# Low-part subtractions moved in attention and in the second recurrence, and a half square moved from VectorE to ScalarE and Pool

## The chip, the cores and the metric

The kernel runs on one NeuronCore of a Trainium2 chip. The metric is the device time of one execution in microseconds, and lower is better. Engines are named as in the profile: PE is TensorE (PEld its weight loads), DVE is VectorE, ACT is ScalarE, POOL is GpSimd, and SP is the queue that issues the weight loads.

## What is computed

The reference is a decoder trunk for 256 tokens of width 1024, all in float32. It has two layers:

```
x = x + rg_lru_block(rmsnorm(x))        # conv, gates, recurrence, output projection
x = x + swiglu(rmsnorm(x))              # dense, width 2816
k, v, c = shared_kv(rmsnorm(x))         # keys, values, summed log forget gates
x = x + fox_attention(rmsnorm(x), k, v, c)   # 16 heads of 64, causal, sigmoid output gate
x = x + moe(rmsnorm(x))                 # top 2 of 8 experts, width 3584
return rmsnorm(x)
```

The recurrence is h[t] = a[t] h[t-1] + b[t] for each of 1024 channels. rmsnorm divides each token by the root of its mean square plus 1e-6. Attention computes, for each head, softmax(q.k / 8 + c[t] - c[s]) over the past, times v, times the gate.

## The kernel before

**Weights in units.** All weight matrices are read as units of 1 MB (128 partitions x 2048 columns), numbered in the order in which TensorE uses them. SP loads unit u into one of six slots of raw. To keep float32 precision with the fast matmul type, every product is made of three: ScalarE rounds the unit to w_hi (split_hi, L400), VectorE makes w_lo = raw - w_hi (split_lo, L751), and TensorE multiplies low by high, high by low and high by high (mm3, L1284 to L1286). w_hi and w_lo have three slots. Activations are split in the same way (act_hi, act_lo, alt_hi, alt_lo).

**Order.** There is no planner. Each engine has its own instruction list, written out by hand, and works through it in order; semaphores join the lists. split_lo(u) waits until ScalarE's count hi_done has reached u + 1, that is until split_hi(u) is done. SP loads unit u + 6 when split_lo(u) is done (lo_done). TensorE starts a unit when its w_lo is there.

**The recurrent block** (units 0 to 11). VectorE handles the eight chunks of channels in two halves. recurrence(h) makes the input of the scan with two elementwise instructions (L892, L894) and runs four scans (L896). After recurrence(1) VectorE runs split_lo(9), then multiplies the result with the gate (gated, L854), with split_lo(10), the low parts (gated_lo, L859), some small constants, split_lo(11) and split_lo(12). Units 8 to 11 are the output projection; TensorE takes units 8 and 9 whole, and units 10 and 11 in two parts, token block 0 first.

**The norm between stages, n = 1 and n = 2.** The 256 tokens are two blocks of 128. For block 1 VectorE adds the first half of the row (add_half, L806), squares and sums it (block1_first_half), takes low parts of block 0 (block_lo, L773), adds the second half, and squares and sums that on top (block1_second_half, L778). Pool raises the mean square to the power -1/2 (inverse_rms, L334). ScalarE scales the second half row (scale_half, L424) and VectorE the first (block1_scale, L802). TensorE transposes the scaled block (transpose_block, L1374), ScalarE rounds it (block_hi, L419) and VectorE makes its low parts. Stage n = 1 leads into the dense layer, n = 2 into keys and values.

**Attention.** Eight passes i = 0 to 7, two heads each, with this list for each engine:

```
PE:   logits(i), transpose_probs(i-1), gate_half(i), values(i-1)
ACT:  out_gate(i-1), probs_T(i-1), exps(i), heads_hi(i-2), split_hi(U_G+2+i/2) if i is even
DVE:  gated_heads(i-2), maxima(i), norms(i), heads_lo(i-2), split_lo(U_G+2+i/2) if i is even
```

maxima (L1046) adds the mask and takes row maxima, exps (L602) exponentiates and sums, norms (L1053, L1056) divides by the sum, transpose_probs (L1541) turns the probabilities, probs_T (L595) copies them to SBUF, values (L1563) multiplies by v, gated_heads (L1067) applies the gate. norms(i) waits for p_exp of its pass, transpose_probs(i) waits for p_norm, probs_T(i) for pt_done. gate_half is half a unit of the gate projection and fills TensorE meanwhile. The units split in attention are U_G+2 to U_G+5; the last two of these belong to the output projection, U_O and U_O+1.

Of the kernel before, what the change touches and what calls it, by code (L numbers as in the profile page):

```python
# [18 lines left out]
D = 1024  # L19
# [8 lines left out]
EPS = 1e-6  # L28
# [8 lines left out]
HALF = D // 2  # L37
# [32 lines left out]
def yoco_kernel(nc, x_in, norm_g, lru_w_in, lru_conv_w, lru_conv_b, lru_gate_w, lru_gate_b, lru_lambda,  # L70
# [6 lines left out]
    with ctx:  # L77
# [117 lines left out]
        ms_ready, rms_ready, xs_act_ready, w_part, d_part, hT_done = (sem(n) for n in ("ms_ready", "rms_ready", "xs_act_ready", "w_part", "d_part", "hT_done"))  # L195
        norm_T, act_hi_done, act_lo_done = sem("norm_T"), sem("act_hi_done"), sem("act_lo_done")
# [116 lines left out]
        def _(pool):  # L313
# [17 lines left out]
            def inverse_rms(n):  # L331
                for t in range(NT):
                    pool.wait_ge(ms_ready, 2 * (n - 1) + t + 1)
                    g.tensor_tensor(rstd[:, n, t:t + 1], msq[:, n, t:t + 1], neghalf[:, 0:1], ALU.pow).then_inc(rms_ready, 1)  # L334
# [59 lines left out]
        def _(act):  # L394
# [18 lines left out]
            def block_hi(n, t, gain, hi):  # L413

                for c in range(KD):
                    if c % 2 == 0:
                        act.wait_ge(norm_T, 4 + 8 * (n - 1) + 4 * t + c // 2 + 1)
                    lo = (c % 2) * T + t * P
                    a.activation(hi[:, c, t * P:(t + 1) * P], bank[4 + c // 2][:, lo:lo + P], ACT.Copy,  # L419
                                 scale=cols[:, gain + c:gain + c + 1]).then_inc(act_hi_done, 1)  # L420

# [101 lines left out]
            block_hi(1, 0, R_NORM + KD, act_hi)  # L523
            scale_half(1)
# [31 lines left out]
            block_hi(2, 0, R_KVN, alt_hi)  # L556
            split_hi(U_V + 2)
# [181 lines left out]
        def _(dve):  # L739
# [37 lines left out]
            def mean_square(n, t, part, so_far, into, count_sem=None):  # L777
                ins = v.tensor_tensor_reduce(out=xs[:, t, part], in0=x[:, t, part], in1=x[:, t, part], scale=1.0 / D, scalar=so_far,  # L778
                                             op0=ALU.mult, op1=ALU.add, accum_out=into)
                if count_sem is None:  # L780
                    link(ins)
                else:
                    ins.then_inc(count_sem, 1)

            def block0_norm(n):

                dve.wait_ge(x_added, 4 * (n - 1) + 2)
                mean_square(n, 0, slice(0, D), EPS, msq[:, n, 0:1], ms_ready)
                dve.wait_ge(rms_ready, 2 * n - 1)
                v.tensor_scalar(xs[:, 0, :], x[:, 0, :], rstd[:, n, 0:1], None, ALU.mult).then_inc(xs_ready, 1)  # L790

            def block1_first_half(n):
                dve.wait_ge(x_added, 4 * (n - 1) + 3)
                mean_square(n, 1, slice(0, HALF), EPS, ss[:, n, 1:2])

            def block1_second_half(n):
                dve.wait_ge(x_added, 4 * (n - 1) + 4)
                mean_square(n, 1, slice(HALF, D), ss[:, n, 1:2], msq[:, n, 1:2], ms_ready)
# [89 lines left out]
            def recurrence(h):  # L888
# [5 lines left out]
                link(v.tensor_tensor(xc[:, part, :], rc[:, part, :], xc[:, part, :], ALU.mult))  # L894
                for c in range(4 * h, 4 * h + 4):
                    last = v.tensor_tensor_scan(rc[:, c, :], decay[:, c, :], xc[:, c, :], 0.0, ALU.mult, ALU.add)  # L896
# [26 lines left out]
            recurrence(1)  # L923
            split_lo(9)
# [30 lines left out]
            block1_second_half(1)  # L955
# [42 lines left out]
            block1_second_half(2)  # L998
# [76 lines left out]
            for i in range(NPH):  # L1075
                if i >= 2:
                    gated_heads(i - 2)
                maxima(i)
                norms(i)
                if i >= 2:  # L1080
                    heads_lo(i - 2)
                if i % 2 == 0:
                    split_lo(U_G + 2 + i // 2)
# [684 lines left out]
```

## Time and profile before

| | |
|---|---|
| median of 3 runs | 1418.53 us (1417.25 to 1419.8) |
| profiled execution, its own time | 1418.73 us |
| its span | 1417.0 us |
| PE busy | 1389.7 us, 98% |
| DVE busy | 1123.2 us, 79% |
| ACT busy | 937.2 us, 66% |
| POOL busy | 55.5 us, 4% |

The profile is that of one execution. Its span runs from the first to the last instruction, and the execution's own time is 1.73 us longer. A row of a timeline gives start and duration in microseconds, the engine, the line of the kernel, the operation, the tile written and the tiles read, and in brackets the idle time of the engine ahead of it with what ended it. Matmuls are pipelined and their ends are modelled, so a row of PE can be longer than the distance to the next one.

### The profile page before, as it was taken

The numbers are of one execution on the slowest core, as the hardware profiler recorded it, in microseconds if no ns is written. First come the engines' busy times: TensorE is split into PE (matmuls) and PEld (weight loads), VectorE is DVE, ScalarE is ACT, GpSimd is POOL, SyncE is SP. The second block draws the span as 40 slices with busy tenths as digits, with TensorE's granted clock in tenths as the row PEclk, the third lists the DMA queues.
The fourth block names the chain that finished last, engine by engine and source line by source line (L and its number), as shares of the span: only waits on it lengthen the run. The fifth ranks groups of instructions, "written<-read, shape, count | busy, mean of one in ns | idle before, by whom it ended". The sixth has DMA issues, their size and how long they took to land.

```text
span 1417.0 us, 19751 instructions
## 1 busy us (share of the span) xinstructions
PE 1389.7 (98%) x7327; PEld 1190.2 (84%) x7327; DVE 1123.2 (79%) x878; ACT 937.2 (66%) x738; POOL 55.5 (4%) x77
## 2 busy tenths in 40 slices
PE   8989999999999999999999999999999999999997
PEld 7979999979878888888788888888888888888885
DVE  7885445576657988888898888888889888888995
ACT  5853343354656777777777777777777777777773
POOL 2002000002003000000000000000000000003000
PEclk9999999999998999999999999999999999999999
DMA  9547955659343999999999999999999999999991
GB/s 311 198 147 270 354 181 192 190 164 384 136 147 113 409 408 393 381 397 365 350 402 367 357 412 376 366 371 406 375 358 402 379 354 407 381 378 369 413 394 64
DMA packets 147772, 454.26 MB, mean 321 GB/s; under 512 B 7528, under 2 KB 50640, under 8 KB 133360
## 3 DMA queue, kind: packets, MB, share of 16 engines
q1 hardware_dynamic: 139360, 423.65, 80.0%
q0 software_dynamic: 6144, 22.12, 4.1%
q10 hardware_dynamic: 2192, 7.39, 1.3%
q8 instruction: 58, 0.95, 0.3%
q14 instruction: 18, 0.15, 0.0%
HBM read 429.54 MB, written 23.59 MB: 320 GB/s over the span
## 4 chain that ended last, share of the span: by engine, by line
PE 92%; DVE 3%; ACT 3%; issue 1%; DMA 0%; ACTq 0%; DVEq 0%; POOLq 0%; POOL 0%
PE bank L1284 29%; PE bank L1285 29%; PE bank L1286 29%; PE bank L1681 2%; DVE w_lo L751 1%; ACT prob L602 1%; ACT w_hi L400 1%; PE bank L1355 0%; PE bank L1689 0%; DMA rows<-in_lru_lambda 0%; DVE rc L896 0%; PE bank L1541 0%; DVE act_lo L773 0%; PE bank L1633 0%; PE bank L1397 0%
## 5 line engine op out<-in xcount | busy, mean ns | idle before, releaser
L1183 DVE TENSOR_TENSOR w_lo<-raw,w_hi 128x2048 fp32r<-128x2048 f32 x249 | 566.3, 2290 | 73.8 <-ACT w_hi L676 72.4
L676 ACT ACTIVATE w_hi<-raw 128x2048 fp32r<-128x2048 f32 x249 | 475.0, 1917 | 142.2 <-PE bank L1286 132.1
L1284 PE MATMUL bank<-w_hi,act_lo 128*128 128x512 f32 (+1 forms) x752 | 291.6, 388 | 3.4 <-issue 1.4
L1286 PE MATMUL bank<-w_hi,act_hi 128*128 128x512 f32 (+1 forms) x752 | 290.0, 386 | 0.0
L1285 PE MATMUL bank<-w_lo,act_hi 128*128 128x512 f32 (+1 forms) x752 | 289.6, 385 | 0.0
L751 DVE TENSOR_TENSOR w_lo<-raw,w_hi 128x2048 fp32r<-128x2048 f32 x67 | 153.2, 2290 | 96.4 <-ACT w_hi L400 96.3
L1183 DVE TENSOR_TENSOR alt_lo<-raw,alt_hi 128x2048 fp32r<-128x2048 f32 x84 | 192.4, 2290 | 37.4 <-ACT alt_hi L676 36.6
L676 ACT ACTIVATE alt_hi<-raw 128x2048 fp32r<-128x2048 f32 x84 | 161.0, 1917 | 43.4 <-PE bank L1286 38.8
L1284 PEld LDWEIGHTS bank<-w_hi,act_lo 128*128 128x128 f32 x752 | 141.9, 189 | 32.9 <-issue 3.3
L1284 PE MATMUL bank<-act_hi,w_lo 128*128 128x256 f32 x576 | 164.8, 286 | 1.9 <-DVE act_lo L763 1.9
L1286 PEld LDWEIGHTS bank<-w_hi,act_hi 128*128 128x128 f32 x752 | 141.5, 188 | 28.4
L1285 PEld LDWEIGHTS bank<-w_lo,act_hi 128*128 128x128 f32 x752 | 141.7, 188 | 27.7
L1285 PE MATMUL bank<-act_lo,w_hi 128*128 128x256 f32 x576 | 162.9, 283 | 0.0
L1286 PE MATMUL bank<-act_hi,w_hi 128*128 128x256 f32 x576 | 162.9, 283 | 0.0
L400 ACT ACTIVATE w_hi<-raw 128x2048 fp32r<-128x2048 f32 x67 | 128.0, 1912 | 38.4 <-PE bank L1286 38.4
L1284 PE MATMUL bank<-w_hi,hid_lo 128*128 128x512 f32 x376 | 148.5, 395 | 0.0
L1285 PE MATMUL bank<-w_lo,hid_hi 128*128 128x512 f32 x376 | 147.8, 393 | 0.0
L1286 PE MATMUL bank<-w_hi,hid_hi 128*128 128x512 f32 x376 | 146.7, 390 | 0.0
L1284 PEld LDWEIGHTS bank<-act_hi,w_lo 128*128 128x128 f32 x576 | 109.9, 191 | 3.1 <-issue 1.5
L1285 PEld LDWEIGHTS bank<-act_lo,w_hi 128*128 128x128 f32 x576 | 109.9, 191 | 0.5
L1286 PEld LDWEIGHTS bank<-act_hi,w_hi 128*128 128x128 f32 x576 | 109.9, 191 | 0.0
L1284 PE MATMUL bank<-alt_hi,act_lo 128*128 128x512 f32 x240 | 94.5, 394 | 0.0
(283 smaller groups left out, 1675.9 us busy)
## 6 DMA issues: line engine op xcount, KB each, us to landing
raw<-in_moe_w_gu SPq DMA_DIRECT2D x224, 1024.0 KB, 7.6
raw<-in_moe_w_down SPq DMA_DIRECT2D x112, 1024.0 KB, 7.8
raw<-in_mlp_w_gu SPq DMA_DIRECT2D x22, 1024.0 KB, 5.2
raw<-in_mlp_w_down SPq DMA_DIRECT2D x11, 1024.0 KB, 5.0
raw<-in_lru_w_in SPq DMA_DIRECT2D x8, 1024.0 KB, 12.7
tok_rows<-zeros POOLq DMA_DIRECT2D x16, 512.0 KB, 17.2
raw<-in_w_kvf SPq DMA_DIRECT2D x8, 1024.0 KB, 5.4
raw<-in_fox_w_qg SPq DMA_DIRECT2D x8, 1024.0 KB, 5.5
```

What stands on the lines that cost most here:

```text
L400: a.activation(w_hi[:, u % SPL, :], raw[:, u % RAW, :], ACT.Copy).then_inc(hi_done, 1)
L602: a.activation(prob[:, b, cut], prob[:, b, cut], ACT.Exp, scale=-1.0, bias=negmax[:, b, t:t + 1], accum_out=psums[:, b, t:t + 1]).then_inc ...
L676: a.activation(moe_slot(g)[0], raw[:, u % RAW, :], ACT.Copy).then_inc(hi_done, 1)
L751: v.tensor_tensor(w_lo[:, u % SPL, :], raw[:, u % RAW, :], w_hi[:, u % SPL, :].bitcast(f32), ALU.subtract).then_inc(lo_done, 1)
L1183: v.tensor_tensor(lo, raw[:, u % RAW, :], hi.bitcast(f32), ALU.subtract).then_inc(lo_done, 1)
L1284: t_.matmul(dst, l_lo, r_hi, start=start, stop=False)
L1285: t_.matmul(dst, l_hi, r_lo, start=False, stop=False)
L1286: return t_.matmul(dst, l_hi, r_hi, start=False, stop=stop)
L1681: last = t_.transpose(banks2[3][:, n * P:(n + 1) * P], hid_rows[:, n // 2, n % 2, :], ident[:])
```

## The change

In attention, split_lo of the even passes goes from the end of the pass to the place between maxima and norms. In the second recurrence, split_lo(9) goes from behind the scans to the place between the second elementwise instruction and the first scan. In the norms n = 1 and 2, the square and sum of the second half row of token block 1 leaves VectorE: ScalarE squares it with a scale of 1/32 and sums it into ss[:, n, 0:1], and Pool adds the two halves before it takes the power. mean_square loses the arguments that nobody needs any longer.

```diff
@@ -193,6 +193,7 @@
         lam_abs, lam_exp = sem("lam_abs"), sem("lam_exp")
         sq_act, sq_dve, msq_ready, rstd_ready, xs_ready = (sem(n) for n in ("sq_act", "sq_dve", "msq_ready", "rstd_ready", "xs_ready"))
         ms_ready, rms_ready, xs_act_ready, w_part, d_part, hT_done = (sem(n) for n in ("ms_ready", "rms_ready", "xs_act_ready", "w_part", "d_part", "hT_done"))
+        sq_half, ms_added = sem("sq_half"), sem("ms_added")
         norm_T, act_hi_done, act_lo_done = sem("norm_T"), sem("act_hi_done"), sem("act_lo_done")
         link_v = sem("link_v")
         tap_ready, xc_ready, gates_done, half_ready = (sem(n) for n in ("tap_ready", "xc_ready", "gates_done", "half_ready"))
@@ -331,6 +332,10 @@
             def inverse_rms(n):
                 for t in range(NT):
                     pool.wait_ge(ms_ready, 2 * (n - 1) + t + 1)
+                    if t:
+                        pool.wait_ge(sq_half, n)
+                        g.tensor_tensor(msq[:, n, 1:2], ss[:, n, 0:1], ss[:, n, 1:2], ALU.add).then_inc(ms_added, 1)
+                        pool.wait_ge(ms_added, n)
                     g.tensor_tensor(rstd[:, n, t:t + 1], msq[:, n, t:t + 1], neghalf[:, 0:1], ALU.pow).then_inc(rms_ready, 1)
 
             g.memset(zeros[:], 0.0).then_inc(zeros_ready, 1)
@@ -418,6 +423,10 @@
                     lo = (c % 2) * T + t * P
                     a.activation(hi[:, c, t * P:(t + 1) * P], bank[4 + c // 2][:, lo:lo + P], ACT.Copy,
                                  scale=cols[:, gain + c:gain + c + 1]).then_inc(act_hi_done, 1)
+
+            def square_half_row(n):
+                act.wait_ge(x_added, 4 * n)
+                a.activation(xs[:, 1, HALF:], x[:, 1, HALF:], ACT.Square, scale=1.0 / 32, accum_out=ss[:, n, 0:1]).then_inc(sq_half, 1)
 
             def scale_half(n):
                 act.wait_ge(rms_ready, 2 * n)
@@ -521,6 +530,7 @@
 
 
             block_hi(1, 0, R_NORM + KD, act_hi)
+            square_half_row(1)
             scale_half(1)
             block_hi(1, 1, R_NORM + KD, act_hi)
             split_hi(U_FF + LEAD)
@@ -554,6 +564,7 @@
 
             split_hi(U_V + 1)
             block_hi(2, 0, R_KVN, alt_hi)
+            square_half_row(2)
             split_hi(U_V + 2)
             scale_half(2)
             block_hi(2, 1, R_KVN, alt_hi)
@@ -774,28 +785,20 @@
                                            scalar=cols[:, gain + c:gain + c + 1], in1=hi[:, c, t * P:(t + 1) * P].bitcast(f32),
                                            op0=ALU.mult, op1=ALU.subtract).then_inc(act_lo_done, 1)
 
-            def mean_square(n, t, part, so_far, into, count_sem=None):
-                ins = v.tensor_tensor_reduce(out=xs[:, t, part], in0=x[:, t, part], in1=x[:, t, part], scale=1.0 / D, scalar=so_far,
-                                             op0=ALU.mult, op1=ALU.add, accum_out=into)
-                if count_sem is None:
-                    link(ins)
-                else:
-                    ins.then_inc(count_sem, 1)
+            def mean_square(n, t, part, into):
+                v.tensor_tensor_reduce(out=xs[:, t, part], in0=x[:, t, part], in1=x[:, t, part], scale=1.0 / D, scalar=EPS,
+                                       op0=ALU.mult, op1=ALU.add, accum_out=into).then_inc(ms_ready, 1)
 
             def block0_norm(n):
 
                 dve.wait_ge(x_added, 4 * (n - 1) + 2)
-                mean_square(n, 0, slice(0, D), EPS, msq[:, n, 0:1], ms_ready)
+                mean_square(n, 0, slice(0, D), msq[:, n, 0:1])
                 dve.wait_ge(rms_ready, 2 * n - 1)
                 v.tensor_scalar(xs[:, 0, :], x[:, 0, :], rstd[:, n, 0:1], None, ALU.mult).then_inc(xs_ready, 1)
 
             def block1_first_half(n):
                 dve.wait_ge(x_added, 4 * (n - 1) + 3)
-                mean_square(n, 1, slice(0, HALF), EPS, ss[:, n, 1:2])
-
-            def block1_second_half(n):
-                dve.wait_ge(x_added, 4 * (n - 1) + 4)
-                mean_square(n, 1, slice(HALF, D), ss[:, n, 1:2], msq[:, n, 1:2], ms_ready)
+                mean_square(n, 1, slice(0, HALF), ss[:, n, 1:2])
 
             def block1_scale(n):
                 dve.wait_ge(rms_ready, 2 * n)
@@ -885,13 +888,15 @@
                 v.scalar_tensor_tensor(out=xc[:, part, :], in0=i_sb[:].rearrange("p j c n -> p (j c) n"), scalar=1.0, in1=xc[:, part, :],
                                        op0=ALU.add, op1=ALU.mult).then_inc(bx_done, 1)
 
-            def recurrence(h):
+            def recurrence(h, between=None):
                 part = slice(4 * h, 4 * h + 4)
                 dve.wait_ge(sqrt_done, h + 1)
                 dve.wait_ge(bx_done, h + 1)
                 link(v.scalar_tensor_tensor(out=rc[:, part, :], in0=decay[:, part, :], scalar=1.0, in1=th[:, part, :],
                                             op0=ALU.add, op1=ALU.mult))
                 link(v.tensor_tensor(xc[:, part, :], rc[:, part, :], xc[:, part, :], ALU.mult))
+                if between:
+                    between()
                 for c in range(4 * h, 4 * h + 4):
                     last = v.tensor_tensor_scan(rc[:, c, :], decay[:, c, :], xc[:, c, :], 0.0, ALU.mult, ALU.add)
                 link(last)
@@ -920,8 +925,7 @@
             gated(1)
             gated_lo(0)
             gated_lo(1)
-            recurrence(1)
-            split_lo(9)
+            recurrence(1, lambda: split_lo(9))
             gated(2)
             gated(3)
             split_lo(10)
@@ -952,7 +956,6 @@
             block_lo(1, 0, R_NORM + KD, act_hi, act_lo, range(0, 4))
             dve.wait_ge(unit_used, U_OUT + 4)
             add_half(1, 1)
-            block1_second_half(1)
             block_lo(1, 0, R_NORM + KD, act_hi, act_lo, range(4, 8))
             block1_scale(1)
             block_lo(1, 1, R_NORM + KD, act_hi, act_lo)
@@ -995,7 +998,6 @@
             add_half(1, 1)
             block_lo(2, 0, R_KVN, alt_hi, alt_lo, range(2, 4))
             split_lo(U_V + 1)
-            block1_second_half(2)
             block_lo(2, 0, R_KVN, alt_hi, alt_lo, range(4, 8))
             block1_scale(2)
             split_lo(U_V + 2)
@@ -1076,11 +1078,11 @@
                 if i >= 2:
                     gated_heads(i - 2)
                 maxima(i)
+                if i % 2 == 0:
+                    split_lo(U_G + 2 + i // 2)
                 norms(i)
                 if i >= 2:
                     heads_lo(i - 2)
-                if i % 2 == 0:
-                    split_lo(U_G + 2 + i // 2)
             gated_heads(NPH - 2)
             heads_lo(NPH - 2)
             gated_heads(NPH - 1)
```

## Rows read from the trace of the kernel before

**Rows 1.** stretches: bounds, length, busy of PE, PEld, DVE, ACT, POOL; clock; DMA

```profile
359.00:410.00 51.00, 46.73 (x401) 39.90 (x400) 32.28 (x122) 33.93 (x93) 1.07 (x2) 0.97 0.38 125
...
450.00:1400.00 950.00, 948.65 (x4300) 787.51 (x4299) 835.23 (x436) 705.10 (x420) 18.55 (x9) 1.00 0.97 375
```

**Rows 2.** waits, 355 to 410 us; columns: total, times, longest

```profile
PEld bank L1541 <- DVE prob L1056: 6.0, 5, 2.1
```

**Rows 3.** DVE timeline in attention: start, duration, line, tiles, [idle before]

```profile
366.98 0.28 DVE L1046 CUSTOM_DVE_ANT_0 prob<-mask,bank 128x128 f32<-128x128 f32 x1
...
374.32 0.18 DVE L1053 RECIPROCAL pinv<-psums 128x4 f32<-128x4 f32 x1 [2.13 <-ACT prob L602]
...
376.43 2.29 DVE L751 TENSOR_TENSOR w_lo<-raw,w_hi 128x2048 fp32r<-128x2048 f32 x1 [0.55 <-ACT w_hi L400]
...
378.64 0.41 DVE L1067 SCALAR_TENSOR_TENSOR q_T<-xs,bank 128x256 f32<-128x256 f32 x1
...
381.53 0.18 DVE L1053 RECIPROCAL pinv<-psums 128x4 f32<-128x4 f32 x1 [1.38 <-ACT prob L602]
```

**Rows 4.** ACT timeline in attention, pass 2

```profile
371.73 0.81 ACT L595 ACTIVATE prob_T<-bank 128x768 f32<-128x768 f32 x1 [1.95 <-PE bank L1541]
...
374.49 1.90 ACT L400 ACTIVATE w_hi<-raw 128x2048 fp32r<-128x2048 f32 x1
```

**Rows 5.** PE timeline in attention: transposes of passes 0 to 3 and 7

```profile
364.42 0.88 PE L1541 MATMUL bank<-ident,prob 128*128 128x128 f32 x6
...
370.82 0.87 PE L1541 MATMUL bank<-ident,prob 128*128 128x128 f32 x6 [0.77 <-DVE prob L1056]
...
376.38 0.87 PE L1541 MATMUL bank<-ident,prob 128*128 128x128 f32 x6
...
382.80 0.87 PE L1541 MATMUL bank<-ident,prob 128*128 128x128 f32 x6 [0.81 <-DVE prob L1056]
...
406.78 1.27 PE L1541 MATMUL bank<-ident,prob 128*128 128x128 f32 x6 [1.89 <-DVE prob L1056]
```

**Rows 6.** stretches on PE: bounds, length, busy, granted clock (share of full)

```profile
407.00:407.50 0.50, 0.50 (x5) 0.60 1.01 393
...
410.50:411.00 0.50, 0.50 (x4) 0.98 0.00 0
```

**Rows 7.** timelines of PE and DVE at the recurrent block's output projection

```profile
75.12 0.50 PE L1284 MATMUL bank<-w_hi,alt_lo 128*128 128x512 f32 x1 [1.69 <-DVE w_lo L751]
...
80.97 2.27 DVE L751 TENSOR_TENSOR w_lo<-raw,w_hi 128x2048 fp32r<-128x2048 f32 x1
...
83.42 0.40 PE L1284 MATMUL bank<-w_hi,alt_lo 128*128 128x512 f32 x1
```

**Rows 8.** timelines of ACT, DVE and PE at the norm n = 1

```profile
91.36 2.17 ACT L419 ACTIVATE act_hi<-bank,cols 128x128 fp32r<-128x128 f32 x8 [0.28 <-PE bank L1374]
...
93.85 0.75 DVE L778 CUSTOM_DVE_ANT_0 xs<-x,ss 128x512 f32<-128x512 f32 x1
...
94.93 0.39 PE L1284 MATMUL bank<-w_hi,act_lo 128*128 128x256 f32 x1 [0.68 <-DVE act_lo L773]
...
96.47 1.03 PE L1374 MATMUL bank<-ident,xs 128*128 128x128 f32 x8
```

**Rows 9.** timelines of DVE and PE at the norm n = 2

```profile
288.25 0.75 DVE L778 CUSTOM_DVE_ANT_0 xs<-x,ss 128x512 f32<-128x512 f32 x1
...
289.42 0.47 PE L1284 MATMUL bank<-w_hi,alt_lo 128*128 128x512 f32 x1 [1.63 <-DVE alt_lo L773]
```

**Rows 10.** groups of instructions of POOL: count, busy us, mean ns, idle before

```profile
L334 POOL TENSOR_TENSOR rstd<-msq,neghalf 128x1 f32<-128x1 f32 x4 | 2.2, 551 | 236.3 <-DVE msq L778 236.3
...
L380 POOL TENSOR_TENSOR zeros<-neghalf 128x2 f32<-128x2 f32 x1 | 1.7, 1692 | 830.7 <-DMA y_rows<-y_sb 830.7
```

**Rows 11.** ACT: one half-row square (timeline), and one table load (groups)

```profile
426.24 0.63 ACT L636 ACTIVATE xs<-x 128x512 f32<-128x512 f32 x1 [2.96 <-DVE x L806]
...
L538 ACT ACT_TABLE_LOAD x1 | 1.3, 1283 | 0.0
```

## The prediction

> **What bounds the kernel now.** First the table of stretches: in the expert stage, 450 to 1400 us, TensorE is busy for 948.65 of 950 us at full clock [rows 1]. Nothing in the diff touches that stage, so the change can only act ahead of it, where TensorE stands idle. The largest such place is attention, where it is busy for 46.73 of 51 us [rows 1]. The waits name the cause: the load of the transposes of the probabilities (L1541) waits 6.0 us in five times for VectorE's normalised probabilities (L1056) [rows 2]. The timelines say how that comes about. In every pass VectorE takes maxima, ScalarE exponentiates, VectorE normalises, TensorE transposes. The normalising of pass 2 starts at 374.32, as soon as ScalarE's exponentials end. After these ScalarE rounds a weight unit, 374.49 to 376.39 [rows 4], and VectorE starts that unit's low part at 376.43, having idled 0.55 us for the rounding [rows 3]. At 378.64 it goes on with pass 3. So the high part is always later than the exponentials of its own pass: it stands behind them on ScalarE's queue. TensorE needs pass 2's probabilities only at 376.38 and waits 0.77 to 1.89 us in the odd passes' transposes [rows 5].
>
> **Attention, the part that decides.** The diff moves split_lo from behind norms(i) and heads_lo(i-2) to a place ahead of both, in the even passes. It adds no work, and ScalarE's order is unchanged. But VectorE works in order, and split_lo waits for a rounding that is queued behind the pass's exponentials. So norms(i) now waits for the rounding as well as the exponentials, and then for the subtraction's 2.29 us. Every wait behind it moves: norms feeds the transposes, these feed ScalarE's copy, and ScalarE does that copy ahead of the next exponentials.
>
> Let T(i) be the start of pass i's transposes, worked out leg by leg.
> - Pass 0: norms starts where maxima(1) starts now, at 366.98 [rows 3]. From the reciprocal to the transposes it takes 382.80 - 381.53 = 1.27 us [rows 3, 5]. T(0) = 368.25 instead of 364.42 [rows 5], 3.83 us late.
> - Even to odd pass: here TensorE's own work binds, transposes, a gate half, values and logits: 376.38 - 370.82 = 5.56 us [rows 5]. The norms of the odd pass are ready sooner, at 374.32 - 370.82 = 3.50 us plus 1.27 = 4.77 us.
> - Odd to even pass: copy, exponentials, rounding, subtraction, norms. Measured from the transposes, VectorE is done with the subtraction after 378.64 - 370.82 = 7.82 us [rows 3, 5]; with 1.27 that is 9.09 us, against TensorE's 5.56. TensorE idles for 3.53 us.
> - Three such pairs: T(6) = 368.25 + 3 x 14.65 = 412.20. Pass 7 follows after 4.77 us (no logits are left to do): T(7) = 416.97 instead of 406.78 [rows 5]. **Warm sum: + 10.19 us.**
>
> heads_lo is also passed by the subtraction, but its results are first read by the output projection. The weight loads that lo_done releases on SP's queue belong to units six further on; in attention the DMA share is 0.38 [rows 1], so I cost their shift at nothing. Without that cover each would cost its own delay, which is within the pair's 14.65 us.
>
> **The clock.** At pass 7 an idle time of 1.89 us ahead of TensorE's transposes [rows 5] was followed by a granted clock of 0.60, then of 0.50 (1.2 GHz), from about 407.1 to 410.5 [rows 6]. That stretch of 3.4 us did 1.7 us less work. The 1.69 us idle in the recurrent block was followed by no fall. An idle of 3.53 us is nearly twice the one that was followed by a fall, so I expect a fall in each of the four even passes, and the one at pass 7 gone, since there TensorE no longer waits. TensorE's own leg of 5.56 us follows each fall and binds, so the loss passes through. Bounds: 1.7 us where the low stretch begins with the work again, 0.85 where half of it lies within the idle time. I take 1.4, nearer to the first, since the one fall shown began 0.3 us after work resumed. 4 x 1.4 - 1.7 = **+ 3.9 us** (from + 1.7 to + 5.1).
>
> **Second recurrence.** split_lo(9) goes ahead of the scans. TensorE now waits 1.69 us for it, until 75.12 [rows 7], and that wait goes. What is late next: the rest of VectorE's list, from gated(2) to split_lo(11), is as long as before, because the scans take the place of the subtraction. split_lo(11) still ends at 80.97 + 2.27 = 83.24, and TensorE took up that unit at 83.42 [rows 7]. It can't be earlier than 83.24. Gain 0, at most 0.2; the idle moves on by one unit.
>
> **Norm n = 1.** VectorE's second half square, 0.75 us at 93.85, goes. TensorE idled 0.68 us just ahead of 94.93 for the low parts behind it [rows 8], so its first part can end some 0.7 us sooner than 96.47, at 95.8. The transposes that follow need the scale. ScalarE has finished its roundings at 91.36 + 2.17 = 93.53 [rows 8] and waits for the addition, so its square runs from about 93.9; 0.63 us plus the reading of the sum [rows 11] makes it 94.6. Then Pool, add and power. A power took 0.55 us; the only add of two small tiles shown took 1.69 [rows 10]. I take 0.55 for the add, since it is nearest in size to the powers, and 0.1 for its semaphore: 95.9, then VectorE's scaling, 0.5: 96.4, against 96.47 now. Sum 0; with an add of 0.2 us a gain of 0.4, with 1.69 a loss of 1.1. A table load before the square would add 1.28 [rows 11]; I cost it at nothing, since the square at 426.24 runs without one behind exponentials. The Trainium skill ("GPSIMD Engine Reference", Key points) says that Pool shares its SBUF interfaces with VectorE and contends with instructions that read two SBUF operands. By that the 1.69 would be an add that met such a subtraction, and here, where VectorE reads PSUM and then waits, the short price would hold. The Trainium skill ("ScalarE: Activation LUTs", Table sets) names copy, relu, identity and abs as in every set, and not the square; by that a load of 1.28 us is possible behind the Gelu, and no row here shows that pair.
>
> **Norm n = 2.** The same square, at 288.25, stands just ahead of the low parts for which TensorE idled 1.63 us until 289.42 [rows 9]. They come sooner by the square less its overlap, some 0.7 us. Between them and the transposes that need the scale lie as many matmuls as in the 1.54 us from 94.93 to 96.47 [rows 8], with twice the columns, so an estimated 2.5 to 3 us: Pool's path, 1.2 to 2.4 us long, is hidden with either price. The added square does hold up what is queued behind it on ScalarE, the rounding of the next value unit, by 0.8 us; VectorE comes to that unit only after its own scaling, so it isn't late. Behind Pool's new wait stands nothing but the power and then stores of zeros, which nobody needs before the experts. **Gain 0.7 us** (0 to 0.8).
>
> **Sum.** Profiled execution 1418.73 us (span 1417.0 and 1.7 around it), within 0.2 of the median 1418.53. 1418.73 + 10.19 + 3.9 + 0 + 0 - 0.7 = **1432.1 us.**
>
> **Rivals.**
> - The clock holds through the idle times. For: 1.69 us of idle left it alone. Against: 1.89 did not. Then 10.19 - 1.7 - 0.7: 1426.5 us.
> - The clock stays low for a second stretch after each fall, as the four idle times recur in every 15 us. Each costs 1.7 more: 1432.1 + 6.8 = 1438.9. Against: the one fall shown was over after 3.4 us [rows 6].
> - Faster: the rounding is done before maxima(i) ends, so the subtraction fills VectorE's 1.4 to 2.1 us idle ahead of the reciprocals [rows 3] and the odd passes start sooner. That would remove 0.77 + 0.81 + 0.81 + 1.89 us of idle [rows 5], the third taken like the second, and the fall, 1.7: 1418.73 - 6.0 - 0.7 = 1412.0. It decides from the point where ScalarE's rounding starts by the time it now starts its copy, 371.73 [rows 4], instead of 374.49. Only a reordered ScalarE queue gives that, and the diff has none.
> - The move has no effect, the subtraction being covered in some way that I don't see: 1418.0.
>
> **Chances.** Forecast 77%, clock holds 8%, clock stays low 12%, faster 2%, no effect 1%. The forecast's own range is 1429.3 (+ 1.7 for the clock, a gain of 0.4 at n = 1) to 1435.0 (+ 5.1, a loss of 1.1 at n = 1, 0 at n = 2: 1435.1). The range for 8 in 10 takes in the warm case and part of the long low one: 1426.5 to 1437. A measurement of this kernel tells 0.2% or 2.8 us from no change. Faster 0.02, within 0.01, slower 0.97.
>
> **What would show it.** In attention of the changed kernel: w_lo ahead of the reciprocal in the even passes, transposes of even passes some 14.7 to 16.4 us apart instead of 12.0, TensorE idle about 3.5 us before each of them, a clock of 0.5 after, none after pass 7; in the recurrence the 1.69 us wait gone and one of about 1.3 us before the unit of split_lo(11); at n = 2 the 1.63 us wait at about 1. A distance of 12 us or less between even transposes would make the forecast wrong, and so would a rounding that ends before the exponentials.

## The result and the profile after

The change makes the kernel slower: 1436.40 us (median of 4 runs, 1433.73 to 1438.69) against 1418.57 us (1417.25 to 1419.80). The ratio is 1.0124, 95% interval 1.0111 to 1.0138. The forecast was 1432.1 us in a range of 1426.5 to 1437.0. The direction and the path of the waits were right; the loss was 17.8 us where 13.4 were forecast, mainly because each fall of TensorE's clock lasted twice as long as was taken.

The profiled execution took 1437.81 us. From its page, to be set beside the table of before:

```profile
span 1436.1 us, 19754 instructions
...
PE 1399.1 (97%) x7327; PEld 1199.6 (84%) x7327; DVE 1121.7 (78%) x874; ACT 938.9 (65%) x742; POOL 56.4 (4%) x79
```

TensorE has only 9.4 us more busy time than before, though the span is 19.1 us longer: it waits more, and part of its work runs at the low clock. The table of stretches (columns as in [rows 1]) puts the loss in attention:

```profile
359.00:420.00 61.00, 46.85 (x350) 41.16 (x347) 30.18 (x114) 28.63 (x79) 1.06 (x2) 0.80 0.26 90
...
468.00:1418.00 950.00, 947.43 (x4291) 786.34 (x4290) 833.65 (x435) 703.73 (x418) 17.89 (x9) 1.00 0.97 375
```

Attention now ends some 18 us later; TensorE is busy for 46.85 of 61 us at a mean granted clock of 0.80, where it was 46.73 of 51 at 0.97 [rows 1]. The 51 us of before reach past pass 7's transposes; the 61 us here end ahead of them, so they hold less of the same work. The expert stage is nearly as it was; what differs stands below.

**Attention.** VectorE's timeline of pass 2 shows the new order, the rows to compare with [rows 3]:

```profile
380.57 2.29 DVE L762 TENSOR_TENSOR w_lo<-raw,w_hi 128x2048 fp32r<-128x2048 f32 x1 [4.30 <-ACT w_hi L405]
...
382.78 0.17 DVE L1055 RECIPROCAL pinv<-psums 128x4 f32<-128x4 f32 x1
```

The subtraction stands ahead of the reciprocal, and VectorE idles 4.30 us for ScalarE's rounding where it idled 0.55. ScalarE's timeline of the same pass shows why [rows 4]:

```profile
375.87 0.82 ACT L606 ACTIVATE prob_T<-bank 128x768 f32<-128x768 f32 x1 [2.31 <-PE bank L1543]
...
377.84 0.50 ACT L613 ACTIVATE prob<-prob,negmax 128x256 f32<-128x256 f32 x1
...
378.64 1.90 ACT L405 ACTIVATE w_hi<-raw 128x2048 fp32r<-128x2048 f32 x1
```

ScalarE copies, exponentiates until 378.4 and only then rounds, from 378.64 to 380.54. The norms could have begun at 378.4; they begin at 382.78. On TensorE's timeline the transposes of passes 0, 1, 2, 6 and 7, for [rows 5], are:

```profile
367.22 1.54 PE L1543 MATMUL bank<-ident,prob 128*128 128x128 f32 x6 [3.76 <-DVE prob L1058]
...
374.96 0.88 PE L1543 MATMUL bank<-ident,prob 128*128 128x128 f32 x6
...
384.05 1.54 PE L1543 MATMUL bank<-ident,prob 128*128 128x128 f32 x6 [3.47 <-DVE prob L1058]
...
417.97 1.54 PE L1543 MATMUL bank<-ident,prob 128*128 128x128 f32 x6 [3.46 <-DVE prob L1058]
...
424.82 0.87 PE L1543 MATMUL bank<-ident,prob 128*128 128x128 f32 x6
```

Ahead of each even pass's transposes TensorE idles 3.46 to 3.76 us, ahead of the odd ones not at all. Even passes are 384.05 - 367.22 = 16.83 us apart, before 11.96. TensorE in half microseconds (columns as in [rows 6]) shows the clock around pass 0:

```profile
365.00:365.50 0.50, 0.00 (x0) 0.76 0.00 0
...
365.50:366.00 0.50, 0.00 (x0) 0.50 0.00 0
...
372.00:372.50 0.50, 0.50 (x5) 0.91 0.00 0
```

It falls at about 365.3, while TensorE still idles, and is back at about 372.1, 6.8 us later. In the other even passes it falls at 382.3, 399.4 and 416.5, each time within TensorE's idle time and each time for 6.8 us. The one fall of before lasted 3.4 us [rows 6].

**The recurrence.** TensorE's waits ahead of units 10 and 11, for [rows 7]:

```profile
79.26 0.47 PE L1286 MATMUL bank<-w_hi,alt_lo 128*128 128x512 f32 x1 [0.36 <-DVE alt_lo L862]
...
83.34 0.50 PE L1286 MATMUL bank<-w_hi,alt_lo 128*128 128x512 f32 x1 [1.09 <-DVE w_lo L762]
```

The wait of 1.69 us ahead of unit 9 is gone. In its place stand 0.36 and 1.09 us, and unit 11 starts at 83.34, before at 83.42.

**The norms.** ScalarE's square at n = 1, Pool's adds at n = 1 and n = 2, then TensorE's transposes at n = 1 and its matmul behind the low parts at n = 2, for [rows 8, 9]:

```profile
93.79 0.63 ACT L429 ACTIVATE xs<-x 128x512 f32<-128x512 f32 x1 [0.23 <-DVE x L809]
...
94.67 0.19 POOL L337 TENSOR_TENSOR msq<-ss 128x1 f32<-128x1 f32 x1 [5.67 <-ACT xs L429]
...
286.17 1.87 POOL L337 TENSOR_TENSOR msq<-ss 128x1 f32<-128x1 f32 x1 [4.77 <-ACT xs L429]
...
96.06 1.09 PE L1376 MATMUL bank<-ident,xs 128*128 128x128 f32 x8 [0.30 <-DVE xs L805]
...
288.40 0.47 PE L1286 MATMUL bank<-w_hi,alt_lo 128*128 128x512 f32 x1 [1.04 <-DVE alt_lo L784]
```

At n = 1 the transposes start at 96.06, before at 96.47; at n = 2 TensorE goes on at 288.40, before at 289.42. So the stages up to 288 us gain 1.0 us. The square runs behind the Gelu without a table load: ScalarE's last load ahead of it, at 69.61, is that of the Gelu itself.

**Behind attention.** TensorE's clock is low once more before the experts begin, at the router (which picks them), in both kernels and in every profile below. In the kernel before (bounds, length, busy, granted clock, DMA share, GB/s):

```profile
434.00:437.80 3.80, 3.80 (x34) 1.00 0.42 169
...
437.80:451.50 13.70, 13.67 (x54) 0.50 0.00 1
```

TensorE had no idle time ahead of this fall; most of its work there was matmuls of 8 columns. The low stretch is 13.7 us long in both kernels, so it doesn't enter their difference, but it varies in the kernels below, and a part of their differences is due to it.

**The expert stage.** In the profiled execution one wait stands out:

```profile
PEld bank L1286 <- DVE w_lo L1185: 3.0, 1, 3.0
```

At the third turn of the expert loop a weight load waited for 3.0 us. TensorE went on at 945.10, and its clock was then low for 3.4 us. The profile names VectorE's subtraction as what ended the wait, but that had ended at 944.12, so the last microsecond has another cause that isn't known. The kernel before has a wait of 1.19 us at another turn instead. From the first full-width matmul of the expert stage to the end of the span it took 1436.1 - 464.87 = 971.2 us, before 1417.0 - 448.62 = 968.4. In the profiles below this stage takes 967.8 to 971.6 us. A wait at this very turn, with a fall of the clock behind it, is in all three profiles of kernels that have the new order in every even pass and neither dummies nor the early rounding. But the one with the norms as before, in which TensorE hardly waits in attention, shows the like at another turn and takes 971.3 us. Whether these 2.8 us belong to the change is open, and they aren't counted as its effect.

### The profile page after: what moved, and what is told of

It reads as the page before. It is cut to its first block, busy times and chain, and to the rows that moved or that the text cites. A ratio compares the mean times of both kernels' runs of the same rounds, so it can differ in the third digit from the quotient of the medians.

```text
span 1436.1 us, 19754 instructions
## 1 busy us (share of the span) xinstructions
PE 1399.1 (97%) x7327; PEld 1199.6 (84%) x7327; DVE 1121.7 (78%) x874; ACT 938.9 (65%) x742; POOL 56.4 (4%) x79
## 4 chain that ended last, share of the span: by engine, by line
PE 92%; DVE 4%; ACT 2%; issue 1%; DMA 0%; ACTq 0%; DVEq 0%; POOL 0%; POOLq 0%
PE bank L1286 29%; PE bank L1287 29%; PE bank L1288 29%; PE bank L1683 2%; DVE w_lo L762 2%; ACT w_hi L405 1%; PE bank L1543 1%; ACT prob L613 1%; PE bank L1691 0%; PE bank L1357 0%; DVE rc L901 0%; DMA rows<-in_lru_lambda 0%; PE bank L1565 0%; DVE prob L1058 0%; PE bank L1635 0%
## 5 line engine op out<-in xcount | busy, mean ns | idle before, releaser
L1286 PE MATMUL bank<-act_hi,w_lo 128*128 128x256 f32 x576 | 168.4, 292 | 1.2 <-DVE act_lo L774 1.2
L1287 PE MATMUL bank<-act_lo,w_hi 128*128 128x256 f32 x576 | 166.0, 288 | 0.0
L1288 PE MATMUL bank<-act_hi,w_hi 128*128 128x256 f32 x576 | 165.9, 288 | 0.0
L1286 PEld LDWEIGHTS bank<-act_hi,w_lo 128*128 128x128 f32 x576 | 113.7, 197 | 2.5 <-DVE act_lo L774 1.1
L1287 PEld LDWEIGHTS bank<-act_lo,w_hi 128*128 128x128 f32 x576 | 113.4, 197 | 0.5
L1288 PEld LDWEIGHTS bank<-act_hi,w_hi 128*128 128x128 f32 x576 | 113.1, 196 | 0.0
```

The costliest lines, as they stand in the source:

```text
L1286: t_.matmul(dst, l_lo, r_hi, start=start, stop=False)
L1287: t_.matmul(dst, l_hi, r_lo, start=False, stop=False)
L1288: return t_.matmul(dst, l_hi, r_hi, start=False, stop=stop)
```

## The experiments

Each was set beside the kernel before on the same chip: 1418.75 us (median of 19 runs) for the first four kernels, 1419.11 (10 runs) for the early rounding and for the subtraction in the odd pass, 1418.87 (9 runs) for the fewer dummies and for the last three. Theory A is the forecast's: norms held up behind the rounding, plus the clock.

### Attention's old order in the changed kernel

```diff
                 maxima(i)
-                if i % 2 == 0:
-                    split_lo(U_G + 2 + i // 2)
                 norms(i)
                 if i >= 2:
                     heads_lo(i - 2)
+                if i % 2 == 0:
+                    split_lo(U_G + 2 + i // 2)
```

> The changed kernel with attention's old order (subtraction behind norms and heads_lo), the other two parts kept. Theory A (the whole loss is attention's order): about 1417.5 us, 1 us under the kernel before; attention is entered some 1.0 us earlier, and its passes take what they took before. Theory B (a good part of the loss is in the recurrence and the norms, or in what they do to later stages): 1421 us or more.

Measured: 1417.31 us (10 runs), ratio 0.9990, interval 0.9979 to 1.0002. Transposes are 6.40 and 5.55 us apart again, and the idle ahead of pass 7 is the old one:

```profile
406.30 1.05 PE L1543 MATMUL bank<-ident,prob 128*128 128x128 f32 x6 [1.89 <-DVE prob L1058]
```

So the whole loss goes with attention's order. The gain of the other two parts, 1 us by the traces, is within what the runs can't tell from nothing.

### Attention's new order alone, on the kernel before

> The kernel before with attention's new order alone. Theory A: about 1437.4 us, 1 us over the changed kernel; even transposes 16.9 us apart. Theory B (the parts only lose together, or attention alone costs the warm sum of 10.2): about 1429 us.

The edit is the reverse of the one above, on the kernel before. Measured: 1436.29 us (1430.05 to 1439.61), ratio 1.0109 (1.0079 to 1.0138). Transposes of passes 0 and 2:

```profile
368.99 1.54 PE L1541 MATMUL bank<-ident,prob 128*128 128x128 f32 x6 [3.76 <-DVE prob L1056]
...
385.88 1.54 PE L1541 MATMUL bank<-ident,prob 128*128 128x128 f32 x6 [3.46 <-DVE prob L1056]
```

They are 16.89 us apart with the same idle times. This and the run above bracket the cause from both sides. The 1 us that this kernel should be over the changed one doesn't show in the medians, 1436.29 and 1436.40, and can't with four executions that span 9.6 us. The shortest of them, 1430.05 us, had a mean granted clock of 0.990, the others 0.983 to 0.985; as a low clock runs at half, its clock was low for an estimated 20 us less (1430 x 2 x 0.007). So not every execution has all the falls that the profile shows; there is no profile of the short one.

### The new order in pass 4 alone

```diff
                 maxima(i)
+                if i == 4:
+                    split_lo(U_G + 2 + i // 2)
                 norms(i)
                 if i >= 2:
                     heads_lo(i - 2)
-                if i % 2 == 0:
+                if i % 2 == 0 and i != 4:
                     split_lo(U_G + 2 + i // 2)
```

> The kernel before with the subtraction ahead of the norms in pass 4 alone. Theory A, dependences plus clock: the transposes of pass 4 come 3.5 us late, those of pass 5 2.7 us late plus about 2.3 us for the low clock; the fall at pass 7 stays; about 1423.5 us. Rival (the loss needs the repetition, as falls of the clock only come where idle times recur every 15 us): 2.7 us, about 1421.3 us. Rival (the move costs the subtraction's own 2.3 us in each pass and nothing else): 1420.9 us.

Measured: 1422.63 us, ratio 1.0029 (1.0019 to 1.0039), 3.9 us over the kernel before. The transposes of passes 3 to 7:

```profile
383.17 0.87 PE L1543 MATMUL bank<-ident,prob 128*128 128x128 f32 x6 [0.81 <-DVE prob L1056]
...
392.25 1.41 PE L1543 MATMUL bank<-ident,prob 128*128 128x128 f32 x6 [3.46 <-DVE prob L1056]
...
399.35 0.87 PE L1543 MATMUL bank<-ident,prob 128*128 128x128 f32 x6
...
404.90 0.87 PE L1543 MATMUL bank<-ident,prob 128*128 128x128 f32 x6
...
411.34 0.88 PE L1543 MATMUL bank<-ident,prob 128*128 128x128 f32 x6 [1.89 <-DVE prob L1056]
```

From pass 3 to 4 it takes 9.08 us (the forecast's leg was 9.09), from 4 to 5 7.10 instead of 5.56: a fall of the clock that costs 1.54 us. From 5 to 6 all is as before. One move is enough for a wait and for a fall. The clock's part was smaller than expected: here it fell when work resumed, at about 392.25, and was low for 3.4 us, not 6.8. The sum over these legs is (9.08 + 7.10) - (5.56 + 6.43) = 4.2 us. Another part of the expectation failed: the idle time of 1.89 us ahead of pass 7 is there, but the clock stays at 1.00 behind it, where it fell in the kernel before. That gives some of the loss back: the first full-width matmul of the expert stage comes 451.68 - 448.62 = 3.1 us late. The median's 3.9 us fit the 4.2 in part by chance, as the profiled execution lost 1.8 us more in the expert stage.

### TensorE kept busy while it waits

```diff
             def transpose_probs(i):
+                if i % 2 == 0:
+                    if i:
+                        pe.wait_ge(pt_ready, i)
+                    keep_warm(7, 2)
                 pe.wait_ge(p_norm, i + 1)
```

keep_warm(7, 2) issues seven matmuls of ones, 256 columns each, into bank 2, which the transposes then overwrite.

> The changed kernel with seven dummy matmuls of 256 columns on TensorE ahead of each even pass's transposes, into the bank that these overwrite, while it waits for the norms. Theory A (10.2 us of the loss are dependences, the rest is the clock): the granted clock stays at 1.0 through attention, even transposes 14.65 us apart, 16.9 now; transposes of pass 7 some 9.2 us after those of the kernel before, and with that kernel's own fall gone about 1426.5 us. Rival (the longer passes come from ScalarE and VectorE, whatever TensorE's clock): still 16.9 us apart and about 1436 us.

Measured: 1427.99 us, ratio 1.0071 (1.0054 to 1.0088). The dummies of pass 2, the transposes of passes 0, 2 and 7, then the stretch of attention (bounds, length, busy, granted clock, DMA share, GB/s):

```profile
367.58 0.87 PE L1547 MATMUL bank<-ident,prob 128*128 128x128 f32 x6 [0.54 <-DVE prob L1058]
...
378.69 3.29 PE L1357 MATMUL bank<-ones 128*128 128x256 f32 x14
...
382.22 0.87 PE L1547 MATMUL bank<-ident,prob 128*128 128x128 f32 x6 [0.25 <-DVE prob L1058]
...
416.28 0.88 PE L1547 MATMUL bank<-ident,prob 128*128 128x128 f32 x6 [0.23 <-DVE prob L1058]
```

```profile
359.00:420.00 61.00, 59.48 (x460) 1.00 0.31 104
```

The clock stays at 1.00, and even passes are 382.22 - 367.58 = 14.64 us apart, 14.65 by the forecast's legs. This splits the loss in attention. From VectorE's first maxima (before and changed) to the transposes of pass 7:

```profile
360.39 0.29 DVE L1046 CUSTOM_DVE_ANT_0 prob<-mask,bank 128x128 f32<-128x128 f32 x1 [2.13 <-PE bank L1532]
...
359.37 0.29 DVE L1048 CUSTOM_DVE_ANT_0 prob<-mask,bank 128x128 f32<-128x128 f32 x1 [2.13 <-PE bank L1534]
```

it takes 406.78 - 360.39 = 46.4 us before, 424.82 - 359.37 = 65.4 changed, and 416.28 - 359.73 = 56.6 with TensorE kept busy. So of the 19.1 us more 10.2 are the waits of VectorE and ScalarE, which dummy work can't shorten, and 8.9 are the clock. The medians say nearly the same, 1436.4 - 1428.0 = 8.4 us for the clock, but they hold more than attention: here the low stretch at the router was 17.1 us long instead of 13.7.

### Fewer dummies: how much idle costs the clock

The same edit with keep_warm(3, 2).

> The changed kernel with three dummy matmuls (1.3 us of work) ahead of each even pass's transposes instead of seven, so that some 2.1 us of idle are left. Open: what length of idle costs the clock here. Theory A (an idle time of 1.9 to 2.1 us is enough only in some positions, as of the idle times of 1.7 to 1.9 us of the kernel before one was followed by a fall and others not): falls in some of the four passes, time between 1428.0 (seven dummies) and 1436.4 (none), passes with a fall 1.6 to 2.3 us longer than the 14.65. Rival (any idle time of two us costs it): a fall in each, about 1435 us.

Measured: 1428.30 us, ratio 1.0066 (1.0049 to 1.0083). Transposes of passes 2, 4 and 6, then the half microsecond in which the clock is low:

```profile
381.31 0.88 PE L1547 MATMUL bank<-ident,prob 128*128 128x128 f32 x6 [1.98 <-DVE prob L1058]
...
395.95 1.04 PE L1547 MATMUL bank<-ident,prob 128*128 128x128 f32 x6 [1.98 <-DVE prob L1058]
...
412.10 0.87 PE L1547 MATMUL bank<-ident,prob 128*128 128x128 f32 x6 [1.98 <-DVE prob L1058]
```

```profile
396.50:397.00 0.50, 0.50 (x5) 0.52 0.49 139
```

Idle times of 1.98 us stand ahead of all three, and one of 2.27 us ahead of pass 0. Only the one ahead of pass 4 was followed by a fall, 0.6 us after work resumed; it was over by 400.0. Pass 4 to 6 takes 16.15 us, pass 2 to 4 14.64, so this fall cost 1.5 us. The medians of the two kernels with dummies are only 0.3 us apart; in their profiles the low stretch at the router was 10.2 us long here and 17.1 there, which can hide such a cost. So for an idle time of two microseconds it isn't the length alone that decides. What does, the position in time or the work around it, these runs don't separate.

### The rounding made early on ScalarE, VectorE's order as changed

```diff
                 if i:
                     out_gate(i - 1)
+                if i % 2 == 0:
+                    split_hi(U_G + 2 + i // 2)
+                if i:
                     probs_T(i - 1)
                 exps(i)
                 if i >= 2:
                     heads_hi(i - 2)
-                if i % 2 == 0:
-                    split_hi(U_G + 2 + i // 2)
```

> The changed kernel, VectorE's order as changed, but ScalarE rounds the unit of an even pass before it copies the probabilities and exponentiates. Theory A (it is the rounding's place on ScalarE's queue that makes the changed order slow): transposes 5.56 us apart from pass 1 on, pass 0 about 1 us late; no low clock; about 1413.5 us. Rival (VectorE's order alone is slow, wherever the rounding stands): above 1425 us. Risk: the rounding delays the exponentials of even passes by 0.8 us, which would show as idle ahead of even transposes.

Measured: 1413.53 us, as expected; ratio 0.9959 (0.9944 to 0.9973). ScalarE's rounding and copy in pass 2, and the transposes of pass 7:

```profile
369.12 1.90 ACT L405 ACTIVATE w_hi<-raw 128x2048 fp32r<-128x2048 f32 x1
...
371.52 0.82 ACT L606 ACTIVATE prob_T<-bank 128x768 f32<-128x768 f32 x1 [0.50 <-PE bank L1544]
```

```profile
403.16 0.87 PE L1544 MATMUL bank<-ident,prob 128*128 128x128 f32 x6 [0.23 <-DVE prob L1059]
```

The rounding now fills ScalarE's idle time ahead of the copy. With VectorE's list exactly as the change has it, the kernel is 5.6 us faster than before instead of 18 slower. So it isn't VectorE's order by itself: it is that order together with the place of the rounding on the other engine's queue. This was the forecast's rival on the fast side; its condition just had to be made true.

### The subtraction in the following odd pass

```diff
                 maxima(i)
-                if i % 2 == 0:
+                if i % 2:
                     split_lo(U_G + 2 + i // 2)
                 norms(i)
```

> The changed kernel with each of the four subtractions put between maxima and norms of the following odd pass, where its rounding is long done and VectorE would idle. Theory A (the place is good only where the rounding is there already): no norms waits for a rounding; all transposes 5.56 us apart; those of pass 7 at about 402.3 us of the span, 4.5 us before the kernel before; no low clock before the end of attention; about 1412.5 us. Rival (any subtraction between maxima and norms delays the probabilities by its 2.3 us): odd transposes late by some 2 us, 1420 us or more.

Measured: 1411.29 us (1410.56 to 1413.07), ratio 0.9944 (0.9926 to 0.9962). VectorE in pass 3, and TensorE's transposes of passes 3 and 7:

```profile
376.01 2.29 DVE L762 TENSOR_TENSOR w_lo<-raw,w_hi 128x2048 fp32r<-128x2048 f32 x1
...
378.29 0.18 DVE L1055 RECIPROCAL pinv<-psums 128x4 f32<-128x4 f32 x1
```

```profile
380.34 0.87 PE L1543 MATMUL bank<-ident,prob 128*128 128x128 f32 x6
...
401.79 0.88 PE L1543 MATMUL bank<-ident,prob 128*128 128x128 f32 x6 [0.24 <-DVE prob L1058]
```

The subtraction starts right after the maxima, without idle, and its 2.29 us fall into the time in which VectorE would wait for the exponentials. Transposes are 5.55 us apart up to pass 6. Those of pass 7 start at 401.79, and no stretch of attention is at the low clock. This version beats both kernels: 7.8 us under the one before.

### The norms as before, on that version

The edit takes the second half square back to VectorE at both norms and drops ScalarE's square and Pool's add.

> The kernel with the subtractions in the following odd pass, but both norms as in the kernel before (second half square on VectorE, no add on Pool). Theory A (the norms are worth 0.3 us at n = 1 and 0.7 us at n = 2, as the changed trace shows by its milestones): attention is entered 1.0 us later than with the new norms, and the whole takes about 1.0 us more, 1412.3 us against 1411.3. Rival (the gain at the milestones is lost again before attention): no difference at attention's start.

Measured: 1413.55 us, 2.3 us over the version above; the two were run on different chips, and their ratios to the kernel before, 0.9961 (0.9949 to 0.9974) and 0.9944 (0.9926 to 0.9962), have overlapping intervals. TensorE at unit 11 and behind the low parts of n = 2:

```profile
83.20 0.50 PE L1290 MATMUL bank<-w_hi,alt_lo 128*128 128x512 f32 x1 [1.07 <-DVE w_lo L756]
...
289.30 0.47 PE L1290 MATMUL bank<-w_hi,alt_lo 128*128 128x512 f32 x1 [1.63 <-DVE alt_lo L778]
```

Between the two milestones lie 206.10 us; in the changed kernel 288.40 - 83.34 = 205.06, and in the version above 205.05. VectorE's first maxima of attention come 277.06 us after unit 11, in the version above 276.02. So the new norms are worth 1.0 us, as expected, and it is still there when attention starts. The rest of the 2.3 isn't theirs. By the traces this kernel was 1.8 us quicker from pass 7's transposes to the experts, as its low stretch at the router was 6.8 us long instead of 13.7, and 3.3 us slower in the expert stage, with an idle time of 2.23 us at 682.2 and a fall of the clock behind it.

### The scans ahead of unit 9's subtraction, on that version

```diff
-            recurrence(1, lambda: split_lo(9))
+            recurrence(1)
+            split_lo(9)
```

> The kernel with the subtractions in the following odd pass, but the second recurrence in its old order (scans, then the subtraction of unit 9). Theory A (VectorE's list up to the subtraction of unit 11 is as long either way, and that sets the start of unit 11): TensorE waits 1.7 us ahead of unit 9 in place of 0.4 and 1.1 us ahead of units 10 and 11; attention is entered at the same time within 0.1 us; 1411.3 us. Rival (the earlier unit 9 is a gain): 1.5 us more.

Measured: 1411.65 us, 0.4 over the version above, which is nothing that these runs can tell. TensorE ahead of unit 9, and VectorE at its first maxima in attention:

```profile
75.32 0.50 PE L1287 MATMUL bank<-w_hi,alt_lo 128*128 128x512 f32 x1 [1.70 <-DVE w_lo L762]
...
359.61 0.29 DVE L1049 CUSTOM_DVE_ANT_0 prob<-mask,bank 128x128 f32<-128x128 f32 x1 [2.13 <-PE bank L1535]
```

The old wait of 1.70 us is back, and none is left ahead of units 10 and 11, as expected. Yet attention is entered at 359.61, in the version above at 359.65. Counted from the start of the second recurrence on VectorE, which itself varies by 0.1 us between the two spans, it is 291.6 us here and 291.5 there. Moving this subtraction bought 0.1 us at most: the idle time lay ahead of unit 9 or was spread ahead of 10 and 11.

### Pool's add away from a subtraction

```diff
-            split_lo(U_V + 1)
             block_lo(2, 0, R_KVN, alt_hi, alt_lo, range(4, 8))
+            split_lo(U_V + 1)
             block1_scale(2)
```

> The changed kernel; at norm n = 2 the subtraction of the unit after U_V goes behind the low parts of chunks 4 to 7, so that Pool's add runs beside VectorE instructions that read PSUM and one SBUF tile. The add took 0.19 us at n = 1, where no subtraction of two SBUF tiles ran beside it, and 1.87 us at n = 2, where one did. Theory A (the add waits for that subtraction): it now takes 0.2 to 0.3 us unless the subtraction starts within it. Rival (n = 2 is slow for Pool's own reasons, say its first instruction after a long idle time or the stores ahead of it): again 1.5 us or more. TensorE gets unit U_V + 1 some 0.8 us later, so the whole is 0 to 1 us longer.

Measured, in one execution: 1439.6 us, which can't be told from the changed kernel's 1433.7 to 1438.7. Pool's add, and TensorE's wait for the unit that is now split later:

```profile
286.31 0.19 POOL L337 TENSOR_TENSOR msq<-ss 128x1 f32<-128x1 f32 x1 [4.76 <-ACT xs L429]
...
289.22 0.50 PE L1286 MATMUL bank<-w_hi,alt_lo 128*128 128x512 f32 x1 [1.72 <-DVE w_lo L762]
```

The add took 0.19 us, where the same add took 1.87 beside the subtraction of two SBUF tiles, in the changed kernel and in all six others above that have the new norms. TensorE goes on 0.7 us later, measured from unit 11 (at 83.48 here), close to the 0.8 expected.

## Why the prediction was right, and where its size was off

**Attention's legs: right to a tenth.** The forecast had 14.65 us for a pair of passes without the clock; with TensorE kept busy 14.64 were measured. It had 9.09 for the odd to even leg; 9.09 were measured (374.96 to 384.05). From the start of attention to the transposes of pass 7 it had a loss of 10.19 us plus the clock's; with TensorE kept busy the loss was 10.2.

**The clock: right in kind, too small.** The forecast took four falls at 1.4 us each, with 1.7 as the bound, for the length of the one fall that it could see. The falls were there, one in each even pass, and the one at pass 7 was gone. But each lasted 6.8 us, not 3.4: it began while TensorE still idled and went on for a good part of its leg. An even to odd leg took 374.96 - 367.22 = 7.74 us in pass 0 and 424.82 - 417.97 = 6.85 in pass 6, against 5.56 and 4.77 without a fall: 2.2 and 2.1 us. The step that failed is the term for the clock, + 3.9 us with + 5.1 as its upper bound. It supposed that a low stretch has the length of the one shown, so that a fall inside the idle time costs less. The sum over attention shows it: the transposes of pass 7 are 424.82 - 406.78 = 18.0 us later. That is 1.0 us of gain, 10.2 of legs, and so 8.8 for the clock, where 5.6 was forecast. The fall of before, now gone, gives back 1.8 us, and 16.25 remain when the expert stage starts (464.87 against 448.62); 13.4 was forecast. The clock's term was thus + 7.0. In the profile the rest lies in the expert stage, 2.8 us, where it isn't explained. The distance of even transposes, 16.8 to 17.0 us, was also past the 14.7 to 16.4 that the forecast named as its sign.

**The rivals.** The clock that holds would have been right only with dummies: that run gave 1428.0 where the rival had 1426.5. The clock that stays low for a second stretch is what happened: 6.8 us low each time, twice the 3.4. The forecast had given it 12%. Its 1438.9 us is also nearer to the measured 1436.4 than the forecast's 1432.1 is. It was too dear, since much of the first stretch lay in the idle time. That the measured time is inside the range is owed to the upper bound, which took in a part of this rival and not only the forecast's own sum. (The lower end of that own sum, 1429.3, should read 1429.5: 1418.73 + 10.19 + 1.7 - 0.7 - 0.4.) The fast rival had the right condition, as the early rounding shows: 1413.5 us, where the forecast's rival had 1412.0.

**The recurrence: right.** Gain 0 was forecast, with the wait moved on. It moved, 0.36 and 1.09 us, where one wait of 1.3 was expected, and the run that undoes the part shows no difference.

**The norms: nearly right.** At n = 1, 0 was forecast with 0.4 for a short add; the add took 0.19 us, and the gain was 0.41 at the transposes (0.34 at the next milestones). At n = 2, 0.7 was forecast and 1.02 - 0.34 = 0.68 came. The Trainium skill ("GPSIMD Engine Reference", Key points) says that Pool contends with VectorE instructions that read two SBUF operands; the trace agrees at both places: 0.19 us where none ran, 1.87 where one did, 0.19 when it was moved away. The forecast's 0.55 for the add, taken from the powers, was too much at n = 1 and too little at n = 2, where either price was hidden, as forecast.

## What to carry to other kernels

Before an instruction is moved into an idle slot of its engine, look at which engine produces its operand and what that producer's instruction is queued behind: a slot that is idle because it waits for X is no slot for work whose input is made after X. Here the same work one pass later, when its input was there, turned a loss of 18 us into a gain of 8. And where a new wait lands on TensorE, price the clock beside it, with the idle time and the work after it both inside the low stretch; here it was nearly half of the loss in attention. Before a difference of 1 or 2 us between medians is put down to an edit, compare the stages that the edit doesn't touch: here they differed by up to 3.8 us from profile to profile.

## What the runs showed of the hardware

- The low clock lasted 6.8 us around idle times of 3.46 to 3.76 us in all four even passes of the changed kernel, and 3.4 us after idle times of 1.89, 1.98 and 3.46 us in three other places (the kernel before, the run with three dummies, the run with one moved pass). In the last the clock held through the idle time and fell when work resumed.
- The same idle time at the same place isn't always followed by a fall: of three of 1.98 us one was, and the 1.89 us ahead of pass 7 was in the kernel before and wasn't in the run with one moved pass.
- The clock also fell with no idle time ahead of it, at the router's matmuls of 8 columns, and was low there for 13.7 us in most profiles, for 6.8 to 17.1 us in others.
- Pool's add of two 128x1 tiles took 0.19 us alone and 1.87 us beside a subtraction of two SBUF tiles on VectorE. The power behind it took 0.55 us in both cases.
- A Square on ScalarE needed no table load though the last load ahead of it was for Gelu_apprx_tanh (n = 1).
